# Opening of a one-core decoder layer: the norm's weight row by products of halves, a new order of three ScalarE and VectorE steps

## The reference, cut to what matters

```python
def rmsnorm(x, g):
    y = x32 * lax.rsqrt(jnp.mean(x32 * x32, axis=-1, keepdims=True) + RMS_EPS)
    return (y * g.astype(jnp.float32)).astype(x.dtype)
...
    h = rmsnorm(x, g_mix_pre)
    proj = h @ w_in          # 1024 x 4608, for 544 tokens
```

## Time and profile before

| | |
|---|---|
| time, median of 3 runs | 761.62 us (760.98 to 761.72) |
| the profiled execution's own time | 761.57 us |
| its span in the trace | 759.7 us |
| PE busy | 751.6 us (99% of the span) |
| DVE busy | 519.8 us (68%) |
| ACT busy | 376.5 us (50%) |
| POOL busy | 116.4 us (15%) |

### The profile page before, as it was taken

How to read it: one execution, slowest core, us unless ns; L and a number is a source line. 1 busy time by engine, 2 the same in 40 slices (tenths; PEclk the granted TensorE clock), 3 DMA queues, 4 the chain that set the end, 5 groups by cost and what they waited for, 6 DMA issues and landing times.

```text
span 759.7 us, 16105 instructions
## 1 busy us (share of the span) xinstructions
PE 751.6 (99%) x5903; PEld 713.0 (94%) x5903; DVE 519.8 (68%) x823; ACT 376.5 (50%) x670; POOL 116.4 (15%) x228
## 2 busy tenths in 40 slices
PE   9999999999999999999999999999999999999996
PEld 6998899898898999997899999999999999999996
DVE  7547737656675574775469887787777899764644
ACT  7334625534733642344466555455554568454442
POOL 6502112020120110003000000000000000453650
PEclk9999999999999999999999999999999999999998
DMA  9645555545543325517461333223332212424274
GB/s 265 164 112 118 151 118 135 149 113 109 153 115 97 95 65 171 167 56 212 147 190 34 112 110 110 85 81 110 110 110 83 84 50 73 137 75 133 69 227 135
DMA packets 185065, 91.77 MB, mean 121 GB/s; under 512 B 52454, under 2 KB 177850, under 8 KB 185020
## 3 DMA queue, kind: packets, MB, share of 16 engines
q1 hardware_dynamic: 178958, 82.69, 39.8%
q0 software_dynamic: 4880, 8.13, 4.0%
q10 hardware_dynamic: 1182, 0.35, 0.2%
HBM read 82.37 MB, written 6.81 MB: 117 GB/s over the span
## 4 chain that ended last, share of the span: by engine, by line
PE 99%; ACT 0%; DVE 0%; DVEq 0%; issue 0%; POOL 0%; POOLq 0%
PE ps L1082 34%; PE ps L1470 28%; PE ps L1587 7%; PE ps L1365 6%; PE ps L1572 5%; PE ps L1534 4%; PE ps L1438 3%; PE ps L1288 2%; PE ps L1189 1%; PE ps L1203 1%; PE ps L1221 1%; PE ps L1263 1%; PE ps L1174 1%; PE ps L1234 1%; PE ps L1116 0%; PE ps L1373 0%
## 5 line engine op out<-in xcount | busy, mean ns | idle before, releaser
L1082 PE MATMUL ps<-xin_hi,w_hi 128*128 128x272 f32 x544 | 117.1, 296 | 0.0
L1082 PE MATMUL ps<-xin_hi,w_lo 128*128 128x272 f32 x544 | 112.6, 288 | 0.0
L1082 PE MATMUL ps<-xin_lo,w_hi 128*128 128x272 f32 x544 | 112.3, 288 | 0.0
L1082 PEld LDWEIGHTS ps<-xin_hi,w_hi 128*128 128x128 f32 x544 | 84.8, 189 | 8.1 <-issue 7.6
L2248 DVE TENSOR_TENSOR w_lo<-w_raw,w_hi 128x1024 fp32r<-128x1024 f32 (+1 forms) x46 | 55.9, 1216 | 47.6 <-ACT w_hi L1662 46.6
L1082 PEld LDWEIGHTS ps<-xin_lo,w_hi 128*128 128x128 f32 x544 | 85.5, 189 | 0.0
L1082 PEld LDWEIGHTS ps<-xin_hi,w_lo 128*128 128x128 f32 x544 | 85.0, 189 | 0.0
L648 POOL DMA_DIRECT2D ytok<-yz x48 | 33.8, 710 | 307.9 <-DVE yz L2809 307.9
L1662 ACT ACTIVATE w_hi<-w_raw 128x1024 fp32r<-128x1024 f32 (+1 forms) x47 | 49.2, 1050 | 47.9 <-PE ps L1082 44.0
L1470 PE MATMUL ps<-xq_lo,b_hi 128*128 128x272 f32 x160 | 46.7, 292 | 0.0
L1470 PE MATMUL ps<-xq_hi,a_lo 128*128 128x272 f32 x160 | 46.4, 290 | 0.0
(11 more groups left out here) (397 smaller groups left out, 2136.6 us busy)
## 6 DMA issues: line engine op xcount, KB each, us to landing
w_raw<-in_w_in_dram SPq DMA_DIRECT2D x68, 256.0 KB, 3.5
g_raw<-in_w_gate_up_dram SPq DMA_DIRECT2D x40, 256.0 KB, 3.8
u_raw<-in_w_gate_up_dram SPq DMA_DIRECT2D x20, 256.0 KB, 3.1
e_raw<-in_w_gate_up_dram SPq DMA_DIRECT2D x20, 256.0 KB, 4.3
raw_p<-in_w_down_dram SPq DMA_DIRECT2D x24, 192.0 KB, 2.5
kc<-in_cache_k_dram SPq DMA_DIRECT2D x64, 64.0 KB
vc<-in_cache_v_dram SPq DMA_DIRECT2D x64, 64.0 KB
raw<-in_w_down_dram SPq DMA_DIRECT2D x12, 320.0 KB, 3.2
```

The source lines that it names most:

```text
L1082: mm = e.matmul(ps[:, bank + h, 0:HT], wt[:, kw, :], xt[:, kx, h * HT:h * HT + HT], start=first and wt is wh and xt is xh, stop=last and ( ...
```

## The change

- The weight row is split in halves: `g_hi` (rounded) and `g_lo` (the rest), with `ones_r`, a rounded copy of the ones. They lie where `xin_lo` will be written later. DVE makes `ones_r`, the first column half of `g_hi` and both halves of `g_lo`; ACT makes the second half of `g_hi`. `g_rows` becomes two fp32r products per column half in place of one 4-byte product.
- The identity transposes in the opening go from 7, 5, 4, 2 to 11, 2, 3, 2.
- DVE makes both `g_copy` before `x_inv(0)`. The bias-table product waits for `norm_step` 5, which is `g_copy(0)`.
- ACT rounds weight 0 before `x_hi` f 0. It no longer copies f 1: DVE does, behind the scaling of tokens 1 and before `x_lo`. The waits on counts follow.

```diff
+    g_hi = put("g_hi", [P, D], F32R, where=w_lo_)
+    g_lo = put("g_lo", [P, D], F32R, where=w_lo_)
+    ones_r = put("ones_r", [P, P], F32R, where=w_lo_)
...
             def g_rows(hf):
-                e.matmul(ps[:, 1 + hf, :], ones[:, :], g_one[:, 512 * hf:512 * hf + 512], start=True, stop=True
-                         ).then_inc(g_spread, 1)
-
-            turn(7)
-            e.wait_ge(consts_v, 6)
-            e.wait_ge(g_in, 16)
+                half = slice(512 * hf, 512 * hf + 512)
+                e.wait_ge(norm_step, 3 + hf)
+                e.matmul(ps[:, 1 + hf, :], ones_r[:, :], g_hi[:, half], start=True, stop=False)
+                e.matmul(ps[:, 1 + hf, :], ones_r[:, :], g_lo[:, half], start=False, stop=True).then_inc(g_spread, 1)
+
+            turn(11)
             g_rows(0)
             g_rows(1)
-            e.wait_ge(norm_step, 1)
+            e.wait_ge(norm_step, 5)
...
             x_T(0, (0,))
-            turn(5)
+            turn(2)
             x_T(0, (1,))
-            turn(4)
+            turn(3)
             x_T(1)
             turn(2)
...
             e.wait_ge(hi_done, 1)
+            e.wait_ge(xt_hi, 2)
+            head_pass(0, 0, w_hi[0], xin_hi, first=True, k1=KD // 2)
             e.wait_ge(xt_hi, 3)
-            head_pass(0, 0, w_hi[0], xin_hi, first=True, k1=KD // 2)
-            e.wait_ge(xt_hi, 4)
+            e.wait_ge(norm_step, 9)
             head_pass(0, 0, w_hi[0], xin_hi, first=True, k0=KD // 2)
...
# ScalarE
+            e.wait_ge(consts_v, 6)
+            e.wait_ge(g_in, 16)
+            e.activation(g_hi[:, 512:D], g_one[:, 512:D], ACT.Copy).then_inc(consts_v, 1)
...
             x_rms(0); x_rms(1)
+            hi(0, 0, 0)
             x_hi(0, (0,))
-            hi(0, 0, 0)
-            x_hi(0, (1,))
             x_hi(1)
...
# VectorE
+            e.wait_ge(consts_v, 6)
+            e.tensor_copy(ones_r[:, :], ones[:, :]).then_inc(norm_step, 1)
+            e.wait_ge(g_in, 16)
+            e.tensor_copy(g_hi[:, 0:512], g_one[:, 0:512]).then_inc(norm_step, 1)
+            e.wait_ge(norm_step, 2)
+            e.tensor_tensor(g_lo[:, 0:512], g_one[:, 0:512], g_hi[:, 0:512].bitcast(F32), ALU.subtract).then_inc(norm_step, 1)
+            e.wait_ge(consts_v, 7)
+            e.tensor_tensor(g_lo[:, 512:D], g_one[:, 512:D], g_hi[:, 512:D].bitcast(F32), ALU.subtract).then_inc(norm_step, 1)
             g_copy(0)
+            g_copy(1)
             x_inv(0)
-            x_scale(0, 2, 0, 512)
-            g_copy(1)
-            x_scale(0, 3, 512, D)
+            x_scale(0, 7, 0, 512)
+            x_scale(0, 7, 512, D)
             x_inv(1)
-            x_scale(1, 4, 0, 512)
-            x_scale(1, 4, 512, D)
+            x_scale(1, 8, 0, 512)
+            x_scale(1, 8, 512, D)
+            e.wait_ge(xt_ready, 2)
+            dst, src = x_fill(xin_hi, 0, 1, 1)
+            e.tensor_copy(dst, src).then_inc(norm_step, 1)
             x_lo(0)
             x_lo(1)
             x_norm(2)
```

More of the change, by code:

```diff
@@ L159, in program @@
     xin_hi = put("xin_hi", [P, KD, T], F32R)
+    xin_lo_at = at[0]
     xin_lo = put("xin_lo", [P, KD, T], F32R)
@@ L223, in program @@
     g_one = put("g_one", [P, D], where=w)
+    w_lo_ = [xin_lo_at]
+    g_hi = put("g_hi", [P, D], F32R, where=w_lo_)
+    g_lo = put("g_lo", [P, D], F32R, where=w_lo_)
+    ones_r = put("ones_r", [P, P], F32R, where=w_lo_)
+    assert w_lo_[0] <= xin_lo_at + 4 * KD * T
     ssum = put("ssum", [P, 8], where=w)
@@ L1315, in _ @@
             head_pass(1, 0, w_lo[1], xin_hi, last=True)
-            e.wait_ge(xt_hi, 9)
+            e.wait_ge(xt_hi, 8)
             head_pass(0, 1, w_hi[0], xin_hi, first=True)
@@ L2275, in x_norm @@
                 x_inv(tt)
-                x_scale(tt, X_ORDER.index(tt) + 3)
+                x_scale(tt, X_ORDER.index(tt) + 8)
             def x_lo(tt):
@@ L2280, in x_lo @@
                     f = X_HALF[tt] + hf
-                    e.wait_ge(xt_hi, f + 1)
+                    if f == 1:
+                        e.wait_ge(norm_step, 9)
+                    else:
+                        e.wait_ge(xt_hi, f + 1 if f == 0 else f)
                     dst, src = x_fill(xin_lo, tt, hf, f)
                     e.tensor_tensor(dst, src, x_fill(xin_hi, tt, hf, f)[0].bitcast(F32), ALU.subtract).then_inc(xt_lo, 1)
+            e.wait_ge(consts_v, 6)
[6 more added lines that the diff above has]
+            e.tensor_tensor(g_lo[:, 512:D], g_one[:, 512:D], g_hi[:, 512:D].bitcast(F32), ALU.subtract).then_inc(norm_step, 1)
             g_copy(0)
+            g_copy(1)
             x_inv(0)
-            x_scale(0, 2, 0, 512)
-            g_copy(1)
-            x_scale(0, 3, 512, D)
+            x_scale(0, 7, 0, 512)
+            x_scale(0, 7, 512, D)
             x_inv(1)
-            x_scale(1, 4, 0, 512)
-            x_scale(1, 4, 512, D)
+            x_scale(1, 8, 0, 512)
[3 more added lines that the diff above has]
+            e.tensor_copy(dst, src).then_inc(norm_step, 1)
             x_lo(0)
@@ L2827, in _ @@
             e.memset(yacc[:, :], 0.0).then_inc(consts_v, 1)
-            e.wait_ge(consts_v, 7)
+            e.wait_ge(consts_v, 8)
             y_square(0, 0)
```

## The result

The changed kernel takes **764.02 us** (median of 21, 761.38 to 766.95), the kernel before 761.62 (21, 760.92 to 763.70): a ratio of **1.0032, 95% interval [1.0022, 1.0042]**, slower by 2.4. The forecast was 761.7 with 760.8 to 762.8, that is next to no change (+0.1), so the size was wrong. One number warns at once: the profiled execution of the changed kernel took 762.08, only 0.51 above that of before. It is the fifth lowest of the 21, and most of the loss isn't in it. The spread tells more: 5.6 us after, 2.8 before.

What follows compares the result with a forecast made beforehand. PE's own work was taken as the bound (99% of the span), with DVE's scaling of the samples setting the opening's end. The profiled 761.57 plus 0.10 gave 761.7, range 760.8 to 762.8.

Steps and rivals of the forecast that it cites:

- ACT's order: ACT rounds weight 0 from 8.93 to 9.98; its opening copies end at 11.8 against 12.11 before.
- DVE's order: In the opening DVE does more between `g_copy(1)` and tokens 1, whose scaling ends at 10.72, 0.5 later than before.
- The rest: Identity transposes, more waits on counts and one higher count near the end cost nothing; no transfer changes place in a queue.
- C's far end: PE's clock rises only beyond 14.5, first passes run at half pace: loss about 2, 763.5 or more; chance 0.07.
- C: Pauses of PE in the opening make its clock rise later, at about 11.2: 762.6, chance 0.16.
- The rule: From the Trainium skill: a DVE copy within SBUF can shut out GpSimd, which writes its DMA descriptors, for the whole instruction.
- rival B: DVE's two new copies push back POOL's parameter loads, the last landing at 13.43 instead of 12.74: 761.75; chance 0.08.
- the row's products: On PE in the opening, four fp32r passes take 1.9 in place of 3.65, from about 4.6.
- rounding the row: DVE rounding 512 columns within SBUF: 0.49 assumed; at its ends, 0.16 and 0.69, the forecast is 761.35 to 761.9.
- `x_lo`: DVE's four steps after its copy of f 1 end at 13.78 instead of 13.06, hidden since PE wants them at about 14.4.
- PE's first product: PE's first real product in the opening starts at about 11.2, not 11.77.
- the samples' scaling: DVE's scaling ends at 19.60, so PE starts the samples' transposes at 19.65, 0.1 later than 19.55.

Runs made afterwards that it cites:

- f1: Changed kernel with one wait added: POOL starts weight 0's low half only after DVE has scaled tokens 1; 763.03 us, ratio 1.0013.
- i1: Changed kernel with only POOL's bias copies held until DVE has made the low halves; 763.44 us, ratio 1.0021.
- h3: Changed kernel with two POOL waits (weight 0's low half, bias copies), idle transposes kept; 761.83 us, ratio 1.0002.
- i4: i1 with five small DVE writes between the halves of tokens 1's scaling, putting the last behind POOL's start; 763.42 us, ratio 1.0019.
- i5: i4 with POOL's subtraction for weight 0's low half held until DVE's scalings are done; 761.87 us, ratio 1.0004.
- e0: Changed kernel unaltered, run again for a second profile; 763.96 us, ratio 1.0043.
- e3: Kernel before with the new ACT and DVE order alone, row's products left as plain 4-byte ones; 765.13 us, ratio 1.0055.
- f3: e3 with POOL's weight 0 low half held until DVE has scaled tokens 1; 761.68 us, ratio 1.0001.
- h2: Kernel before with only POOL's bias copies held until the key weight's low half is made; 761.18 us, ratio 0.9998.
- h4: e3 with two POOL waits, on weight 0's low half and on the bias copies; 761.67 us, ratio 1.0001.
- e1: Changed kernel with plain 4-byte identity products in place of the idle transposes; 763.49 us, ratio 1.0028.
- f2: e1 with POOL's weight 0 low half held until tokens 1 are scaled; 761.38 us, ratio 1.0001 without one far-out time.
- h1: f2 with POOL's bias copies also held until the key weight's low half is made; 762.57 us, ratio 1.0009, in two groups.
- f4: Kernel before with the row's products by halves alone and plain 4-byte products in place of idle transposes; 763.43 us, ratio 1.0023.

## Why the prediction was wrong

| changed kernel | first meeting left | first meeting away |
|---|---|---|
| second left | 764.02, ratio 1.0032 | f1 763.03, 1.0013 |
| second away | i1 763.44, 1.0021 | h3 761.83, 1.0002 |

Each less the before on its own chip is +2.4, +1.5, +1.8 and +0.45, so by the medians the first meeting costs 1.4 by itself, the second 1.1, and both together 1.95. These sizes are rough: the intervals are 0.7 to 1.0 us to each side, and those of f1 and h3 overlap. The first meeting is measured better by i1 or i4 against i5, on one chip: 1.6. For the second, seven of f1's eleven times lie above all of h3's, and the traces show the wait. Without the meetings the changed kernel takes 761.83, near the 761.7 forecast.

*The step that failed is "ACT's order".* It worked out right that weight 0 is rounded at 8.9 (8.80), and it asked only what stood behind that wait on ACT. It didn't ask who else is released by the rounding: POOL's subtraction, which comes up from 10.74 to between 9.6 and 10, onto DVE's last scaling, while "DVE's order" moved that scaling later, toward it (over at 10.53 for 10.21). Each engine's order was sound by itself; the two together closed a gap of 0.53, from 10.21 to 10.74, POOL's row of before above. "The rest … nothing" failed with it: the bias copies began 0.13 behind the parameter steps, and an opening 0.5 late can lose that. It did in e0; in the first profile, just as late, the copies came at 26.79 and missed the steps. In the ten profiles without the bias wait they begin between 25.24 and 26.79, by when their transfer lands.

That 764.02 falls among the times that the prediction gave C's far end (0.07) is chance: C wanted a rise beyond 14.5.

*The rule was at hand*, on the page of the Trainium skill named in the prediction, and was weighed for POOL's descriptors only (rival B). There it costs little: the one issue of POOL beside the new casts took 0.63 instead of 0.51. The last parameter transfer did land later, mostly by its own 6.6 against 5.9; PE's parameter transposes were 0.68 behind before, and weight 1's first pass again only 0.52. What the rule says of a VectorE and a GpSimd instruction that both read SBUF was the point that mattered, and it was not applied.

*PE's clock (C).* The sign was right and the price small: rise at 9.89, samples' transposes 0.53 late instead of 0.1. The seven profiles with the changed kernel's work on PE (after, e0, f1, h3, i1, i4, i5) have the rise at 8.47 to 11.41, the five with the row's 4-byte products (before, e3, f3, h2, h4) at 5.68 to 7.95. By itself that stays within the range: h3 has the changed kernel's work on PE and 761.34 to 762.51. Its harm is that it makes the second meeting likelier.

*Right by their rows:* the row's products from 4.68 (4.6 forecast); `g_copy` at 5.94 and 6.80 (5.97, 6.87); rounding the row 0.42 (0.49 taken of 0.16 to 0.69); tokens 1 scaled by 10.53 (10.72); `x_lo` ended at 13.87 (13.78). *Wrong:* PE's first product, 12.30 for 11.2, as the bias table and the first four transposes behind it ran at the lower level, so that PE, and not the scaling, set the transposes of tokens 0 (9.12, with the first scaling over at 8.34); the samples' scaling, over at 20.02 for 19.60.

**Left open.** Why the clock rises at 5.55 in one profile and at 10.34 in another with the same work on PE (e1, f2). And the upper group of h1, some 1.5 above the lower: it has no profile of its own. i5's profile, at 762.67, may show a part of it. Its lag grows by 0.19 at 431 us and by 0.57 from 440 to 442, the latter behind a weight transfer: DVE, idle 1.55 for it, begins its step on `e_raw` at 437.23, where before has it at 435.65. f1's profile has a wait of 1.8 for the same tile, and a growth of 0.76 at 442 to 444. No version was clearly faster than before.

## What to carry over

When an edit makes a result ready earlier, follow its semaphore to every engine that it releases, and lay what that engine then starts beside what the others do in those microseconds: VectorE with two operands in SBUF and GpSimd reading SBUF should not be due together. If they must be close, fix the order by a wait of the one that nobody waits for, here one line on GpSimd. And when a change widens the spread of the times, the one profiled execution may be a good one: profile again before reading a cause from it.

## What the runs showed of the hardware

- A meeting's price depends on the order: 0.43 for POOL when DVE is first, about 2.1 for a scaling of 0.75 when POOL is first. A transfer that let ACT begin 0.3 earlier (8.48 for 8.80) turned the one into the other, and the opening was 1.86 late instead of 0.53: an earlier load can make it slower.
- Nine DVE steps of 128x4, 1.73 or 1.74 alone, took 2.12 to 3.48 beside POOL's copies. POOL's four copies took 2.48 where they came first (f1) and 3.54 where DVE's low half of 1.22 had begun 0.01 ahead (before).
- PE's granted clock fell back in the opening after pauses of 1.39 and 1.00 (f4), and eight products then took 2.08 instead of some 1.2.
- One DMA issue of POOL took 0.62 or 0.63 in all 12 profiles with DVE's two casts beside it, and 0.51 in all five without.
